# DeltaNet rows spread in PSUM, redone engine orders, and attention values as one group of products per head in a hybrid decoder block

## The reference, cut to what matters

```python
# A: gated DeltaNet, 8 heads of 128
lower = where(strict, einsum('..cd,..sd->..cs', k * beta, k) * decay, 0)
a_mat = lower + eye                 # unit lower triangular, solved per chunk
sol = triangular_solve(a_mat, rhs)
qk = where(tri, einsum('..cd,..sd->..cs', q, k) * decay, 0)
# per chunk: v_new = u - w @ state; o = (q * exp(gc)) @ state + qk @ v_new
#            state = state * exp(g_last) + k_dec^T @ v_new
o_a = o * rsqrt(mean(o * o) + EPS) * gdn_norm_w * silu(z)

# B: forgetting attention, 16 heads of 64
sc = q @ k^T * d**-0.5 + cum_q - cum_k ; sc = where(causal, sc, -inf)
o_b = (softmax(sc) @ v) * sigmoid(fo)

y = sigmoid(mga) * (o_a @ w_branch_a) + sigmoid(mgb) * (o_b @ w_branch_b)
x = x + y @ w_out ; x = x + swiglu(rms_norm(x)) ; out = rms_norm(x)
```

## Time and profile before

| | us |
|---|---|
| median of 3 runs | 1267.2 (1263.39 to 1269.47) |
| the profiled execution | 1270.5 |
| its span, first to last instruction | 1268.8 |
| PE busy | 1206.7 (95%) |
| DVE busy | 549.1 (43%) |
| ACT busy | 429.1 (34%) |
| POOL busy | 472.2 (37%) |

### The profile page before, as it was taken

The page is one execution under the profiler, slowest core; times in us unless marked ns, Lnnn a source line. Parts: engine busy times, 40 slices in busy tenths (PEclk is TensorE's granted clock), DMA queues, the critical chain, the costliest instruction groups (busy, mean ns, idle before and its releaser), DMA issues.

```text
span 1268.8 us, 16828 instructions
## 1 busy us (share of the span) xinstructions
PE 1206.7 (95%) x6093; PEld 999.9 (79%) x6093; DVE 549.1 (43%) x1148; ACT 429.1 (34%) x680; POOL 472.2 (37%) x232
## 2 busy tenths in 40 slices
PE   6999978979979899999999998999999999999997
PEld 5868867868868697888888877888788888888886
DVE  4334455382653823666666654542333333340001
ACT  5344441422424234444334432223322222231222
POOL 6334442250422405233223323443444444443443
PEclk9989987997979999999999998999999999999999
DMA  6223322130211304323333316442233333322231
GB/s 187 76 67 93 99 64 61 47 104 26 75 50 59 92 26 133 84 78 87 91 91 91 91 51 199 133 116 83 84 99 99 99 93 91 97 99 84 100 116 67
DMA packets 169630, 113.57 MB, mean 90 GB/s; under 512 B 6257, under 2 KB 157922, under 8 KB 169586
## 3 DMA queue, kind: packets, MB, share of 16 engines
q1 hardware_dynamic: 163218, 98.26, 26.8%
q10 hardware_dynamic: 6368, 14.72, 3.3%
HBM read 104.54 MB, written 8.42 MB: 89 GB/s over the span
## 4 chain that ended last, share of the span: by engine, by line
PE 62%; issue 19%; DVE 10%; POOL 7%; ACT 1%; DMA 0%; DVEq 0%; POOLq 0%; SPq 0%; ACTq 0%
PE ps L1310 41%; PE ps L1708 9%; PE ps L1393 7%; POOL w_lo L527 6%; DVE Lq L1069 2%; PE ps L1292 2%; DVE rows L1059 1%; PE ps L1354 1%; DVE E L1001 1%; DVE Lq L1044 1%; DVE Wb L1074 1%; DVE Zm L1080 1%; PE ps L1644 1%; DVE tmp L948 1%; PE ps L1382 0%
## 5 line engine op out<-in xcount | busy, mean ns | idle before, releaser
L527 POOL TENSOR_TENSOR w_lo<-raw,w_hi 128x1024 fp32r<-128x1024 f32 x170 | 420.5, 2474 | 754.7 <-ACT w_hi L628 754.7
L1310 PE MATMUL ps<-h_hi,w_lo 128*128 128x512 f32 x976 | 401.9, 412 | 0.0
L1310 PE MATMUL ps<-h_hi,w_hi 128*128 128x512 f32 x976 | 386.5, 396 | 3.6 <-POOL w_lo L527 1.9
L1310 PE MATMUL ps<-h_lo,w_hi 128*128 128x512 f32 x976 | 386.9, 396 | 0.0
L628 ACT ACTIVATE w_hi<-raw 128x1024 fp32r<-128x1024 f32 x170 | 180.1, 1060 | 548.9 <-PE ps L1310 455.6
L1310 PEld LDWEIGHTS ps<-h_lo,w_hi 128*128 128x128 f32 x976 | 184.8, 189 | 39.2 <-issue 1.2
L1310 PEld LDWEIGHTS ps<-h_hi,w_hi 128*128 128x128 f32 x976 | 185.8, 190 | 37.3 <-POOL w_lo L527 3.1
L1310 PEld LDWEIGHTS ps<-h_hi,w_lo 128*128 128x128 f32 x976 | 186.8, 191 | 31.9 <-issue 1.0
L948 DVE SCALAR_TENSOR_TENSOR tmp<-ps,prm,tmp 128x511 f32<-128x511 f32 (+2 forms) x72 | 53.9, 748 | 88.4 <-ACT tmp L658 83.2
L916 DVE TENSOR_SCALAR ms<-ss 128x1 f32<-128x1 f32 x8 | 1.2, 154 | 126.0 <-ACT raw L889 117.4
L1248 DVE TENSOR_TENSOR f_lo<-tmp,f_hi 128x512 f32 (+1 forms) x22 | 40.5, 1841 | 33.7 <-ACT f_hi L862 33.7
(11 more groups left out here) (242 smaller groups left out, 1597.4 us busy)
## 6 DMA issues: line engine op xcount, KB each, us to landing
raw<-in_w_in SPq DMA_DIRECT2D x80, 512.0 KB, 3.8
raw<-in_w_gate SPq DMA_DIRECT2D x22, 512.0 KB, 3.7
raw<-in_w_up SPq DMA_DIRECT2D x22, 512.0 KB, 3.7
raw<-in_w_down SPq DMA_DIRECT2D x22, 512.0 KB, 3.2
gate_dram<-gate ACTq DMA_DIRECT2D x24, 256.0 KB, 2.0
cumb<-cum_dram ACTq DMA_DIRECT2D x8, 512.0 KB, 3.5
raw<-in_w_branch_a SPq DMA_DIRECT2D x8, 512.0 KB, 4.3
raw<-in_w_branch_b SPq DMA_DIRECT2D x8, 512.0 KB, 3.6
```

The costliest lines, as they stand in the source:

```text
L527: pool.tensor_tensor(w_lo[:, r % 2, :], raw[:, r, :], w_hi[:, r % 2, :], ALU.subtract)\
L1310: return pe.matmul(ps[:, bank, :], wts[wl][k], acts[xl][:, k, :], start=(n == 0), stop=(n == len(PASSES) - 1))
```

## The change

In DeltaNet the spread rows lie in PSUM, in banks that stand free then, and the product has a tile of its own. DVE no longer masks all of E, which POOL does (`decay_mask`); DVE cuts the four diagonal quadrants out of E (`decay_cut`), scales them early, and multiplies them by k k^T straight from PSUM. `Zm` is written by eight whole-width pieces, four on DVE and four on ACT, with no zeroing. PE turns the last chunk's output first, and the passes are dealt out anew: before the wait for `Zm` stand 69 passes after q's transposes; 34 follow the next decay. POOL makes the output norm's power ahead of a low half. In attention POOL divides the probabilities by their sums ahead of the transposes (`scale_probs`); scores, transposes and values stand as one group per head; the transposed probabilities are kept as a high half (ACT) and a low half (DVE); v is kept as high and low half side by side in the stationary operand `v2`, so that each matmul of up to 512 columns gives both halves' products, in partitions 0 to 63 and 64 to 127, which DVE adds. The output comes out transposed, so `o_turn` is gone.

```diff
-    FILLS = (14, 8, 4, 30, 26, 5, 5, 4, 5, 4, 4, 4)
+    FILLS = (6, 4, 35, 24, 5, 5, 4, 5, 4, 4, 4)
...
-            ROW_AT[row] = rows[:, col:col + H * (row + 1)].rearrange("p (h n) -> p h n", h=H)
-            col += H * (row + 1)
+        for bank, some in ((4, (1, 2, 3, 4, 5, 6, 7, 8, 10)), (5, (9, 11, 12, 13, 14)), (0, (15,))):
+            col = 0
+            for row in some:
+                ROW_AT[row] = ps[:, bank, col:col + H * (row + 1)].rearrange("p (h n) -> p h n", h=H)
+                col += H * (row + 1)
...
# POOL
+            def decay_mask(c):
+
+                pool.wait_ge(E_cut, 4 * c + 4)
+                pool.tensor_tensor(E[:, :, :], E[:, :, :], low[:, :].unsqueeze(1).broadcast_to([P, H, C]),
+                                   ALU.mult).then_inc(E_masked, 1)
...
                 pool.wait_ge(osc_step, c * 4 + 3)
                 power(osc[:, :], oss[:, :], H).then_inc(osc_pow, 1)
+                ahead(c, 4)
                 if c < TT - 1:
-                    pool.wait_ge(w_done, led(w_done, 2 * c + 2))
-                    pool.memset(Zm[:, :, :], 0.0).then_inc(Z_zero, 1)
...
+            def scale_probs(i):
+
+                for h in range(2):
+                    pool.wait_ge(rsum_ready, 2 * i - 1 + h)
+                    pool.sem_inc(rsum_seen, 1)
+                    for t in range(4 * h, 4 * h + 4):
+                        s = probs[:, START[t]:START[t] + (TASKS[t][1] + 1) * P]
+                        pool.tensor_scalar(s, s, rsum[:, t:t + 1], None, ALU.mult).then_inc(probs_scaled, 1)
...
# ACT
+                act.wait_ge(W_done, c + 1)
+                for b in range(NB // 2, NB):
+                    act.activation(Zm[:, :, b * BS:(b + 1) * BS], Wb[:, :, :], ACT.Copy,
+                                   scale=own_neg[:, b:b + 1]).then_inc(Z_right, 1)
...
+                            act.activation(pT_hi[:, h * NS + a:h * NS + b], ps[:, bank, 0:b - a], ACT.Copy)\
+                                .then_inc(pT_high, 1)
...
# DVE
+                for q in QUADS:
+                    dve.tensor_tensor(Em[q, :, :], E[q, :, q], tri32[q].unsqueeze(1).broadcast_to([2 * BS, H, 2 * BS]),
+                                      ALU.mult).then_inc(E_cut, 1)
...
+                dve.tensor_tensor(Lq[:, :, :], Em[:, :, :], bn2[:, :].unsqueeze(2).broadcast_to([P, H, 2 * BS]),
+                                  ALU.mult).then_inc(Lq_scaled, 1)
...
-                for a in range(2):
-                    for q in QUADS:
-                        dve.tensor_tensor(half(Zm, a)[q, :, q].rearrange("p h (r j) -> p h r j", r=2),
...
+                for b in range(NB // 2):
+                    dve.tensor_scalar(Zm[:, :, b * BS:(b + 1) * BS], Wb[:, :, :], own_neg[:, b:b + 1], None, ALU.mult)\
+                        .then_inc(Z_left, 1)
...
+                        dve.wait_ge(pv_done, 2 * i - 1 + h)
+                        dve.tensor_copy(tmp[h * FD:(h + 1) * FD, 0, :], ps[0:FD, 7 - h, :]).then_inc(o_half, 1)
+                        dve.wait_ge(o_half, 2 * i - 1 + h)
+                        dve.tensor_tensor(tmp[h * FD:(h + 1) * FD, 0, :], tmp[h * FD:(h + 1) * FD, 0, :],
+                                          ps[FD:P, 7 - h, :], ALU.add).then_inc(o_taken, 1)
...
# PE, attention
-                            last = pe.matmul(ps[:, 7, t * FD:(t + 1) * FD], probsT[:, s:s + P],
-                                             v_nat[:, k, h * FD:(h + 1) * FD], start=(k == 0), stop=(k == b))
...
+                        for k in range(TT):
+                            s, n = h * NS + KSTART[k], (TT - k) * P
+                            for at, half_p in enumerate((pT_hi, pT_lo)):
+                                last = pe.matmul(ps[:, 7 - h, k * P:T], v2[:, k, h, :], half_p[:, s:s + n],
+                                                 start=(k == 0 and at == 0), stop=(k == TT - 1 and at == 1))
...
+                        unit(q, 0, h_hi, h_lo, [score(0), score(1)], None, (5, 17))
+                        unit(q, 1, h_hi, h_lo, [probs_turn(0), probs_turn(1)], None, (7, 19))
+                        unit(q, 2, h_hi, h_lo, [values(0), values(1)], None, (6, 18))
...
+                    score(0)()
+                    unit(AB0, 0, a_hi, a_lo, [score(1), probs_turn(0)], None, (8, 20))
+                    unit(AB0, 1, a_hi, a_lo, [probs_turn(1), values(0)], None, (8, 20))
+                    values(1)()
```

More of the change, by code:

```diff
@@ L360, in hybrid_block @@
                 y_sum: 2}
-        for s in (a_low, b_low, b_mul, probsT_ready, o_taken, w_done, of_turned, of_ready, oT_ready, S_ready,
+        for s in (a_low, b_low, b_mul, pT_low, o_taken, w_done, of_turned, of_ready, oT_ready, S_ready,
                   X_ready, o_ready):
@@ L795, in fox @@
                     act.activation(vT[:, :], ps[:, 0, :], ACT.Copy).then_inc(v_taken, 1)
+                if attention:
+                    for h in range(2):
+                        for n, (bank, _) in enumerate(TURNED):
+                            act.wait_ge(probs_turned, 6 * i - 6 + 3 * h + n + 1)
+                            a, b = COLS[n]
+                            act.activation(pT_hi[:, h * NS + a:h * NS + b], ps[:, bank, 0:b - a], ACT.Copy)\
+                                .then_inc(pT_high, 1)
+                if products:
                     high_ahead(q, 1)
@@ L1054, in chunk @@
                     .then_inc(Lc_step, 1)
+                dve.wait_ge(E_masked, c + 1)
+                for a in range(2):
+                    dve.wait_ge(qk_done, c * 2 + a + 1)
+                    dve.tensor_tensor(half(qk, a), bank4(a), half(E, a), ALU.mult).then_inc(qk_ready, 1)
                 dve.wait_ge(Lc_step, c * 2 + 2)
+                dve.wait_ge(Vb_ready, c * 2 + 2)
                 def spread(row):
@@ L1572, in go @@
-                        last.then_inc(probs_turned, 1)
-                    return go
-                def values(t):
-                    h, b = TASKS[t]
+                        else:
+                            pe.wait_ge(pT_low, led(pT_low, 6 * a + 3))
+                        for bank, parts in TURNED:
+                            for k, col in parts:
+                                for b in range(k, TT):
+                                    s = START[h * TT + b] + k * P
+                                    last = turn(ps[:, bank, col + (b - k) * P:col + (b - k + 1) * P], probs[:, s:s + P])
+                            last.then_inc(probs_turned, 1)
@@ L1586, in go @@
[L1586 to L1594 removed]
+                        pe.wait_ge(pT_low, led(pT_low, 6 * a + 3 * h + 3))
+                        if h == 1:
+                            pe.wait_ge(pT_low, led(pT_low, 6 * a + 6))
```

299 lines of the change are left out of this document (142 added, 157 removed).

## The result

The changed kernel takes 1210.9 us in the median of 4 runs (1209.2 to 1214.9), beside 1265.3 us (1262.3 to 1269.5, 4 runs) for the kernel before: a ratio of 0.957, with a 95% interval of 0.955 to 0.960. The forecast was 1209 in a range of 1189 to 1242. The profiled execution took 1211.3 us (forecast 1212.1).

The account below looks back on a forecast made before the run. PE's waits for `Zm` and the slow clock behind them were the largest item, 46.5 us. DeltaNet 42.5, attention 11.9 and last pair 4 took 58.4 from the profiled 1270.5, less 3.3 to the median: 1209 us, range 1189 to 1242.

Parts of the forecast that it names:

- The wait for `Zm` and its clock: DeltaNet chunks: PE's waits for the substitution's result, 22.6 us, and slow clock behind, 23.9; 1.9 us per chunk would remain.
- the sum: DeltaNet's four chunks: 46.5 us for `Zm` and 1.9 for other waits, less 4 x 1.9 remaining, gives 42.5 us.
- That the clock stays up: DeltaNet, behind the remaining 1.9 us wait for `Zm`: the clock holds, read from old waits of 1.7 and 3.7 us.
- The rival of the falling clock: DeltaNet: PE's wait only shrinks to some 3.5 us or more and the clock still falls; 1242 us, chance 0.15.
- That PSUM costs nothing: DeltaNet's substitution: rows in PSUM add nothing per step, at worst 1.5 us a chunk.
- PE's work in an iteration: Attention loop: PE's work per iteration falls to 30.6 us from 33.4.
- DVE's blocked low part: Attention: the output split's low part is blocked 2.4 us by POOL; late minima make second-head scores wait about 1.1 us.
- POOL's scaling: Attention: dividing the probabilities takes POOL 1.9 to 3 us per head, hidden with 3 us to spare.
- the slower rival: Attention: POOL's scaling at S per head breaks even at 7.5 us; at 9 about 1284 us; chance 0.03.
- The last pair: End of attention: values, output turn and a shorter way to `b_low` give 4 us, bounds 2 and 5.
- The total: Whole kernel: DeltaNet 42.5, attention 11.9 and last pair 4 give 58.4 us less, so 1209 us.

Follow-up runs that it names:

- kernel with DeltaNet alone: The changed DeltaNet with the old attention, a part of the change on the kernel before: 1220.3 us, ratio 0.963.
- late split: The changed kernel with DVE's split of a pair's gated output moved behind the next pair's first minima: 1198.4 us, ratio 0.947.
- the kernel with the gates earlier: Late split, plus SP's first gate loads issued once the last pair's values are done, ahead of two weight loads: 1191.4 us, ratio 0.943.

## Why the prediction came out as it did

**The wait for `Zm` and its clock** carried the forecast, and were right. The substitution takes 9.8 us (251.25 to 261.01; forecast 10.0), no product over 0.29. The early scaling won its race at 244.96 against POOL's 244.98, by 0.02 us, and POOL was the one held up (2.15 instead of 1.90); it won in all four chunks (0.42 us in the mean). The quadrants took 1.76 (1.6); Lc wasn't blocked (0.31, where I charged 0.5): it started at 249.49, as POOL's low half ended. From Kd to PE's turns pass 22.4 us (22.9), and PE was there after 21.6 (21.0). So the wait was 0.6 to 0.85 us in three chunks, none in the first, and not 1.9: 5.5 us more gained than in the sum. The waits for Kd, 1.7, which the sum left out, went as well. Against it stand the gate bank's wait, which I had let go and which stayed, a new 1.2 for E, and the cold start of this profile, 5.03 - 2.84 = 2.2. 42.5 + 5.5 + 1.7 - 1.7 - 1.2 - 2.2 = 44.6, beside 45.7 measured. For the kernel with DeltaNet alone, with waits of 3.3 and no such start, it is 42.5 + 4.3 + 1.7 - 1.7 - 1.2 = 45.6, beside 46.5.

**That the clock stays up** was right in its result and wrong in its bound. I took two waits of the old trace, 1.7 and 3.7 us, and put the fall at 3.5. Behind `Zm` it falls at 2.1 already, and behind 1.6 and 0.6 sometimes. No run has a wait of 1.9 us, the one that I forecast; it lies among waits behind which the clock held in one place and fell in another. That the wait came out 1 us shorter, where no profile shows a fall, was luck. The rival of the falling clock deserved more than 0.15.

**That PSUM costs nothing** held to the nanosecond: the form of 128 x 128 took 291 ns from PSUM and 292 from SBUF, the smallest 176 and 177, and the shuffles, which write there, 231 in the mean instead of 232. The Trainium skill's "Perfetto Trace Analysis" (Optimizing Scalar/DVE Operations), with 60 against 125 ns of access overhead, isn't borne out for these instructions.

**PE's work in an iteration**, 30.6 us, was right: 30.63 where nothing is waited for. DVE's blocked low part was right too: 2.0 us above its free time, where I charged 2.4, and 31.43 - 30.63 = 0.8 us lost to late minima where the scaling is left out, forecast 1.1.

**POOL's scaling is the term that failed.** I bounded it at 1.9 to 3 us per head and called it hidden with 3 us to spare. It takes 4.35, and single instructions 0.61 to 1.57 us where I expected 0.3 to 0.9:

```profile
L632 POOL TENSOR_SCALAR probs<-probs,rsum 128x512 f32<-128x512 f32 x16 | 25.1, 1570 | 0.0
...
L632 POOL TENSOR_SCALAR probs<-probs,rsum 128x128 f32<-128x128 f32 x16 | 9.7, 606 | 26.6 <-DVE rsum L1206 26.6
```

These are 0.29 us per instruction and 2.5 ns per element, dearer than the one-operand pass of the earlier trace rows (1.03) and than the product of the earlier trace rows (1.9). Its start was right: 7.5 us into the iteration, as the slower rival had it, with the late minima in it. But I compared only the second head with its turn. With S = 4.35 the first head is ready at 7.5 + 4.35 = 11.9, and its turn is due at 11.4 (read where the scaling is left out); the second is ready at 7.5 + 2 x 4.35 = 16.2 and its turn was forecast at 15.1. Both wait, 0.44 and 0.19 us of idle time. The late split takes the other way out: the scaling is as long, starts at 5.2, and is hidden. PE lost 1.0 us to the scaling and 0.8 to the minima, where I had 1.1 in all, so an iteration gave 1.0 and not 1.7.

**The last pair** was to give 4 us, bounds 2 and 5. Both ends of the attention together gave 2.3 (9.3 less 7 x 1.0). PE waited 1.67 us there for minima and 0.79 for the scaling, which I put down to the 8 passes between its two groups of scores, where the loop has 12; the late split alone took 2.5 us off this stretch (from the last `vT` turn, 42.9 to 40.4). What follows is set by the gates' loads, as the kernel with the gates earlier shows: 4.4 us of wait remained (3.7 before), since `b_low` came 6.8 us ahead of PE's stop and before the change 6.9.

**The slower rival** had a sound rule and a slip in its sum. Its own 10.4 us for each of eight pairs are 83 us and give 1292 at S = 9, not 1284. With S = 9.4 us per head the kernel took 1301.8 us; the rule gives 11.2 us per pair, 1298. It left out that the clock falls in the waits. The real S of 4.35 lay above my bound and below the break-even of 7.5.

**The total** was closer than its parts, by luck: 3.2 us too little for the chunks and 6.6 too much for the attention leave 3.4 too much (4.0 by the medians), and the kernel before lay 1.9 us lower in these runs than in those first shown. In the profiled executions the 4.5 us ahead of DeltaNet, which no step foresaw, closed the gap.

## What to carry over

When a small chain of two-operand DVE work lies beside POOL's, ask where its operands live before reordering anything: one operand moved to PSUM was worth some 28 to 32 of 46 us alone. Leave room above the dearest neighbour when an operation isn't in the trace: at the 2.4 ns per element that the prediction named, 1280 elements are 3.1 us, and four instructions of 0.29 us on top make 4.2, near the 4.35 measured; then compare it with every turn that waits for it, the first as well as the last. A wait behind which the clock can fall costs twice, so aim well under the shortest wait that has cost it in any profile, not just under the shortest one seen in yours.

## What the hardware showed that I had not expected

The granted clock after one and the same wait isn't the same in each profile. Near 70 us all kernels of the study run the same code, with a wait of 2.4 us between passes and small products. From 72 to 78 us the clock is 0.58 in the kernel before and 1.00 in the changed one:

```profile
72.00:78.00 6.00, 6.00 (x9) 0.98 (x8) 1.99 (x3) 0.63 (x1) 1.57 (x1) 0.58 0.39 108
```

```profile
72.00:78.00 6.00, 6.00 (x23) 3.85 (x22) 0.75 (x1) 1.22 (x2) 0.26 (x1) 1.00 0.34 94
```

The same eight products behind the wait take 6.12 us in the one (from 72.00) and 3.61 in the other (from 70.06). In the thirteen profiles the clock of this stretch lies between 0.50 and 1.00, and the stretch up to DeltaNet takes 151.6 to 154.7 us. These are different kernels with the same code in this place; but the one kernel before, measured 13 times beside the first experiments, also ran from 1260.0 us at a mean clock of 0.976 to 1270.7 at 0.968. Two profiles of the same code can thus differ by 3 us in one place; what a change did is better read stage by stage than from two spans.
